# Head norms and first output units moved into the last attention head; convolution taps partly on TensorE, their norm in channel layout

## The reference

```python
def conv_lru_mixer(...):
    h = x @ w_in + b_in                                   # 4 parts of 512: a_val, a_gate, b_gate, b_rec
    ya = silu(layer_norm(causal_depthwise_conv(a_val * sigmoid(a_gate), conv_w, conv_b), cnorm_g, cnorm_b))   # 31 taps
    yb = rg_lru(causal_depthwise_conv(b_rec, lru_conv_w, lru_conv_b), ...) * gelu(b_gate)                   # 4 taps
    return concatenate([ya, yb], axis=-1) @ w_out

def diff_attention_mixer(...):                            # 8 heads, value width 128
    ...                                                   # scores, masked softmax of two maps, p0 - lam * p1, times v
    o = rms_norm(o, subln_g) * (1.0 - lambda_init)        # over the 128 of each head
    return o @ w_out
```

## Time and profile before

| what | value |
|---|---|
| median of 3 runs | 3826.24 us (3825.8 to 3828.29) |
| the profiled execution's own time | 3837.27 us |
| its span | 3835.5 us |
| PE busy | 3571.9 us, 93% |
| DVE, ACT, POOL busy | 48%, 32%, 13% |
| mean granted TensorE clock | 0.95 |

### The profile page before, as it was taken

The page is one execution under the profiler, slowest core; times in us unless marked ns, Lnnn a source line. Parts: engine busy times, 40 slices in busy tenths (PEclk is TensorE's granted clock), DMA queues, the critical chain, the costliest instruction groups (busy, mean ns, idle before and its releaser), DMA issues. The chain is left out here.

```text
span 3835.5 us, 41703 instructions
## 1 busy us (share of the span) xinstructions
PE 3571.9 (93%) x15900; PEld 2867.3 (75%) x15900; DVE 1858.0 (48%) x2465; ACT 1216.6 (32%) x1733; POOL 492.7 (13%) x277
## 2 busy tenths in 40 slices
PE   7847999999998999969999999999988989999998
PEld 5636888888876777638888888888866768888886
DVE  7994623223255666655423233555347865323235
ACT  3225521111133444444411112454422343212123
POOL 0003400000042000006100000442001531000004
PEclk9877999999999999979999999999976989999998
DMA  2101223122122111102222132222221213111113
GB/s 93 38 16 66 88 66 110 52 71 90 48 73 77 45 55 38 38 11 90 91 71 88 49 109 91 96 89 95 72 72 39 82 61 96 58 49 44 49 55 99
DMA packets 75997, 261.14 MB, mean 68 GB/s; under 512 B 10224, under 2 KB 10608, under 8 KB 75888
## 3 DMA queue, kind: packets, MB, share of 16 engines
q1 hardware_dynamic: 75888, 259.69, 21.1%
HBM read 246.54 MB, written 4.72 MB: 66 GB/s over the span
## 5 line engine op out<-in xcount | busy, mean ns | idle before, releaser
L197 PE MATMUL ps<-xh,whi 128*128 128x512 f32 x2880 | 1012.5, 396 | 109.2 <-DVE wlo L628 47.4
L197 PE MATMUL ps<-xl,whi 128*128 128x512 f32 x2880 | 1003.9, 393 | 0.0
L197 PE MATMUL ps<-xh,wlo 128*128 128x512 f32 x2880 | 1002.8, 392 | 0.0
L180 DVE TENSOR_TENSOR wlo<-stage,whi 128x1024 fp32r<-128x1024 f32 x366 | 525.3, 1435 | 507.0 <-ACT whi L174 505.9
L174 ACT ACTIVATE whi<-stage 128x1024 fp32r<-128x1024 f32 x366 | 386.5, 1056 | 1099.6 <-PE ps L197 1068.2
L197 PEld LDWEIGHTS ps<-xh,whi 128*128 128x128 f32 x2880 | 546.9, 190 | 237.0 <-issue 86.2
L197 PEld LDWEIGHTS ps<-xh,wlo 128*128 128x128 f32 x2880 | 546.8, 190 | 115.5
L197 PEld LDWEIGHTS ps<-xl,whi 128*128 128x128 f32 x2880 | 548.2, 190 | 112.7
L197 PE MATMUL ps<-hh,whi 128*128 128x512 f32 x1216 | 422.5, 396 | 5.9 <-ACT lam_t L1477 3.9
L197 PE MATMUL ps<-hl,whi 128*128 128x512 f32 x1216 | 421.2, 395 | 0.0
L197 PE MATMUL ps<-hh,wlo 128*128 128x512 f32 x1216 | 421.2, 395 | 0.0
(11 more groups left out here) (324 smaller groups left out, 3622.9 us busy)
## 6 DMA issues: line engine op xcount, KB each, us to landing
stage<-in_w_ff SPq DMA_DIRECT2D x88, 512.0 KB, 3.5
stage<-in_w_gate SPq DMA_DIRECT2D x59, 512.0 KB, 3.2
stage<-in_w_up SPq DMA_DIRECT2D x59, 512.0 KB, 3.3
stage<-in_w_in SPq DMA_DIRECT2D x50, 512.0 KB, 3.2
ada<-in_w_ada SPq DMA_DIRECT2D x48, 512.0 KB, 3.4
stage<-in_w_qkv SPq DMA_DIRECT2D x43, 512.0 KB, 3.3
stage<-in_w_down SPq DMA_DIRECT2D x48, 448.0 KB, 3.3
stage<-in_w_out SPq DMA_DIRECT2D x32, 512.0 KB, 3.3
```

The source lines that it names most:

```text
L180: dve.tensor_tensor(wlo[slot][:], stage[slot][:], whi[slot][:].bitcast(F32), ALU.subtract).then_inc(w_split, 1)
L197: done = pe.matmul(acc[:, h * HALF:(h + 1) * HALF], wt[slot][:, w], xt[:, b, h * HALF:(h + 1) * HALF], start=b == 0 and wt is whi and xt i ...
```

## The change

In the convolution stage the last 6 taps of each block (in the last block 8 more) become fp32 matmuls with diagonal matrices, which ACT makes from `ident` and the weight columns; the other taps run over all 1024 tokens at a time in two alternating accumulators, and the part from PSUM and the two accumulators are added. The taps are ordered anew, the split of the next block's third unit moves ahead of the scan, and the last block stands outside the loop. `channel_norm` is removed. `ChannelNorm` does the norm for two halves of 512 tokens in channel layout: total, spread_out, deviation, invert and broadcast as in `Norm`, its first half ahead of `out0`, its second half between the first units of `out0` (its totals, its broadcast, and `normalise`, `silu` and `low` on DVE, ACT and POOL). In attention, the block of the head norms is gone. `pe_last`, `act_last` and `dve_last` do the last head, with the norms of heads 0 to 6 and of the first half of head 7, and the first two units of `out1`'s first half between its steps; the low parts go to POOL (`sub_low`). The rest of head 7's norm stands between the units that follow. The three blocks of the program become one.

```diff
-    def channel_norm(name, src, nblk, gain, bias, dst, other):
...
-    TAPS_BEFORE_REC, TAPS_BEFORE_LRU, TAPS_BEFORE_SCAN = 7, 20, 24
+    conv_o = sb("conv_o", [P, S], at=lru_scope)
+    PE_TAPS, LATE_TAPS = 6, 8
+    diag = sb("diag", [P, PE_TAPS, P], at=lru_scope)
+    diag_late = w_gates[:].rearrange("p a k n -> p (a k) n")[:, 0:LATE_TAPS, :]
...
+            def taps_of(i, lo, n, w, to):
+                for t in range(n):
+                    for h in range(2):
+                        at = h * HALF + lo + t
+                        done = pe.matmul(to[:, h * HALF:(h + 1) * HALF], w[:, t, :], a_pad[:, at:at + HALF], start=t == 0, stop=t == n - 1)
+                done.then_inc(tap_mm, 1)
...
-                pe.wait_ge(lru_taps, 2 * LRU_TAPS * i + 2 * LRU_TAPS)
+                pe.wait_ge(diag_ready, i + 1)
+                pe.wait_ge(acc_free, u + 4)
+                taps_of(i, CONV_TAPS - PE_TAPS, PE_TAPS, diag, ps[2])
+                mm_unit(pe, gin0, 2 * i + 1, 1, DB, xh, xl, ready)
+                pe.wait_ge(taps, STEPS * i + WITH_PART + 1)
+                pe.wait_ge(lru_taps, LRU_TAPS * i + LRU_TAPS)
...
+                if last_block(i):
+                    pe.wait_ge(diag_ready, AB + 1)
+                    pe.wait_ge(acc_free, u + 5)
+                    taps_of(i, CONV_TAPS - PE_TAPS - LATE_TAPS, LATE_TAPS, diag_late, ps[0])
...
+            def diagonals(i, lo, n, w):
+                for t in range(n):
+                    done = act.activation(w[:, t, :], ident[:], ACT.Copy, scale=col("conv_w", CONV_TAPS * i + lo + t))
+                done.then_inc(diag_ready, 1)
+            diagonals(0, CONV_TAPS - PE_TAPS, PE_TAPS, diag)
...
+                if last_block(i):
+                    act.wait_ge(gate_w, AB)
+                    diagonals(i, CONV_TAPS - PE_TAPS - LATE_TAPS, LATE_TAPS, diag_late)
+                else:
+                    act.wait_ge(tap_mm, i + 1)
+                    diagonals(i + 1, CONV_TAPS - PE_TAPS, PE_TAPS, diag)
...
+                def conv_steps(n):
+                    for _ in range(n):
+                        k = step[0]
+                        t = k if k < WITH_PART else k - 1
+                        dst = conv_o[:] if k % 2 else out
...
+                        if k == 0:
+                            op = dve.tensor_scalar(dst, a_pad[:, 0:S], col("conv_w", CONV_TAPS * i), col("conv_b", i), ALU.mult, ALU.add)
+                        elif k == 1:
+                            op = dve.tensor_scalar(dst, a_pad[:, 1:1 + S], col("conv_w", CONV_TAPS * i + 1), None, ALU.mult)
+                        elif k == WITH_PART:
+                            dve.wait_ge(tap_mm, i + 1)
+                            op = dve.tensor_tensor(dst, ps[2][:], dst, ALU.add)
+                        else:
+                            op = dve.scalar_tensor_tensor(dst, a_pad[:, t:t + S], col("conv_w", CONV_TAPS * i + t), dst, ALU.mult, ALU.add)
+                        op.then_inc(taps, 1)
+                        step[0] += 1
...
+                conv_steps(6)
...
+                    lru_tap(t)
+                    conv_steps(1)
+                conv_steps(min(SPLIT_AT, n_taps + 1) - step[0])
                 split_lo4(dve, i, 5)
...
+                conv_steps(n_taps + 1 - step[0])
+                done = STEPS * i + n_taps + 1
+                if last_block(i):
+                    dve.wait_ge(decays, 2 * i + 2)
...
+                if not last_block(i):
+                    split_lo4(dve, i, 6)
...
+                    dve.wait_ge(tap_mm, AB + 1)
+                    dve.wait_ge(taps, done + 1)
+                    dve.tensor_tensor(out, ps[0][:], out, ALU.add).then_inc(taps, 1)
...
+        def squares(self, act):
+            for b in range(AB):
+                act.activation(c_sq[:, b, self.t], conv[:, b, self.t], ACT.Square).then_inc(cn_sq, 1)
+        def sums(self, dve):
+            h = self.h
+            for b in range(1, AB):
+                for q, src in enumerate((conv, c_sq)):
+                    to = c_sum[:, h, q, :]
...
+                    dve.tensor_tensor(to, src[:, 0, self.t] if b == 1 else to, src[:, b, self.t], ALU.add).then_inc(cn_sum, 1)
...
+            dst = conv[:, 2 * p:2 * p + 2, self.t]
+            dve.tensor_tensor(dst, dst, wide(BANK_MEAN), ALU.subtract).then_inc(cn_y, 1)
+            dve.wait_ge(cn_y, n + 1)
+            dve.tensor_tensor(dst, dst, wide(BANK_RSTD), ALU.mult).then_inc(cn_y, 1)
...
+        def silu(self, act, p):
+            act.wait_ge(cn_y, 4 * self.h + 2 * p + 2)
+            for b in (2 * p, 2 * p + 1):
+                act.activation(conv[:, b, self.t], conv[:, b, self.t], ACT.Silu, bias=col("cnorm_b", b), scale=col("cnorm_g", b)).then_inc(cn_silu, 1)
+            act.wait_ge(cn_silu, SILU + AB * self.h + 2 * p + 2)
+            act.activation(xh[:, AB + 2 * p:AB + 2 * p + 2, self.t], conv[:, 2 * p:2 * p + 2, self.t], ACT.Copy).then_inc(a_hi, 1)
+        def low(self, eng, p):
+            eng.wait_ge(a_hi, 2 * self.h + p + 1)
+            eng.tensor_tensor(xl[:, AB + 2 * p:AB + 2 * p + 2, self.t], conv[:, 2 * p:2 * p + 2, self.t],
+                              xh[:, AB + 2 * p:AB + 2 * p + 2, self.t].bitcast(F32), ALU.subtract).then_inc(a_lo[self.h], 1)
...
-        run(eng, Head(HEADS - 1), Head(HEADS - 2), False)
...
+    def sub_square(dve, h, k=None):
+        if h == 0:
+            dve.wait_ge(mm_done, gq.base + UPH * HEADS + 2)
+        dve.wait_ge(o_out, NT * h + (NT if k is None else 4 * (k + 1)))
+        o = sub_place(o_t, h, k)
+        dve.tensor_tensor(sub_place(sub_sq_at, h, k), o, o, ALU.mult).then_inc(sub_sq, 1)
+    def sums(pe, h, k):
+        n = 2 * h + k
+        pe.wait_ge(sub_sq, sub_n(h, k if h == HEADS - 1 else None))
...
+        pe.matmul(bank, ones, sub_sq_at[:, h, k * HALF:(k + 1) * HALF], start=True, stop=True).then_inc(sub_mm, 1)
+    def sub_log(act, h, k):
+        act.wait_ge(sub_mm, 2 * h + k + 1)
+        bank = half(ps[0], k) if h < HEADS - 1 else half(ps[0], 1) if k == 0 else half(ps[2], 1)
+        act.activation(sub_rs_at[:, h, k * HALF:(k + 1) * HALF], bank, ACT.Ln, bias=eps[:], scale=1.0 / P).then_inc(sub_ln, 1)
+    def sub_scale(act, h, k=None):
+        act.wait_ge(sub_ln, 2 * h + (2 if k is None else k + 1))
+        r = sub_place(sub_rs_at, h, k)
+        act.activation(r, r, ACT.Exp, scale=-0.5).then_inc(sub_rs, 1)
+    def sub_gain(dve, h, k=None):
+        dve.wait_ge(sub_rs, sub_n(h, k))
+        o = sub_place(o_t, h, k)
+        dve.scalar_tensor_tensor(o, o, lam_t[:, 5:6], sub_place(sub_rs_at, h, k), ALU.mult, ALU.mult).then_inc(sub_o, 1)
+    def sub_high(act, h, k=None):
+        act.wait_ge(sub_o, sub_n(h, k))
+        act.activation(sub_place(xh, h, k), sub_place(o_t, h, k), ACT.Copy).then_inc(sub_hi, 1)
+    def sub_low(eng, h, k=None):
+        eng.wait_ge(sub_hi, sub_n(h, k))
+        eng.tensor_tensor(sub_place(xl, h, k), sub_place(o_t, h, k), sub_place(xh, h, k).bitcast(F32), ALU.subtract).then_inc(sub_lo, 1)
+    def out1_part(pe, u, lo, hi):
+        slot, n = (o1a.base + u) % 2, o1a.base + u
+        if lo == 0:
+            pe.wait_ge(w_split, n + 3)
+            pe.wait_ge(acc_free, n + 1)
+            pe.wait_ge(sub_ln, 2 * (HEADS - 1) + u % 2)
+        for b in range(lo, hi):
+            if u == 0:
+                pe.wait_ge(sub_lo, b + 1)
+            for wt, xt in ((whi, xh), (whi, xl), (wlo, xh)):
+                done = pe.matmul(half(ps[0], u % 2), wt[slot][:, b * P:(b + 1) * P], xt[:, b, 0:HALF],
+                                 start=b == 0 and wt is whi and xt is xh, stop=b == DB - 1 and wt is wlo)
+        if hi == DB:
+            done.then_inc(mm_done, 1)
...
+    def pe_last(pe):
+        def beside(qt, k):
+            if qt in (5, 6):
+                out1_part(pe, qt - 5, 2 * k, 2 * k + 2)
+            if qt == 5 and k == 1:
+                sums(pe, HEADS - 1, 0)
+            if qt == 7 and k < 2:
+                out1_part(pe, k, EARLY_BLOCKS, DB)
+        for qt in range(NT):
+            who, tile = (sixth, NT - 1) if qt == 0 else (last, qt - 1)
+            scores(pe, last, qt)
+            if qt == 1:
+                values_t(pe, last, 1)
+            beside(qt, 0)
+            weights_t(pe, who, tile, 0)
+            beside(qt, 1)
+            weighted(pe, who, tile, 0)
+            if tile >= BATCH:
+                weights_t(pe, who, tile, 1)
+            beside(qt, 2)
+            if tile >= BATCH:
+                weighted(pe, who, tile, 1)
+            if qt == 0:
+                values_t(pe, last, 0)
+            if qt == 1:
+                for h in range(HEADS - 1):
+                    for k in range(2):
+                        sums(pe, h, k)
+        for b in range(2):
+            weights_t(pe, last, NT - 1, b)
+            weighted(pe, last, NT - 1, b)
...
+    def act_last(act):
...
+            if qt == 0:
+                act_values(act, last, 0)
+                split_hi(act, o1a, 0, 1)
+            if qt == 1:
```

(84 more changed lines are left out.)

617 lines of the change are left out of this document (358 added, 259 removed).

## The result

The changed kernel takes **3772.4 us** (median of 4 runs, 3770.9 to 3774.8) against 3826.0 (4 runs, 3825.4 to 3828.3) of the kernel before: ratio 0.9859, 95% interval 0.9842 to 0.9876, 54 us less. The forecast was 3764 in a range of 3745 to 3790, faster with a chance of 0.95. The profiled execution took 3770.9 us, its span is 3769.1. Against the profiled execution of before that is 66 us less, 12 more than the medians say. 11 of them are the excess of that execution of before over its own median, which the forecast took off. It can be placed: past the output product the kernels are the same, and one stretch of 250 us ran at a lower granted clock in the profile of before.

What follows compares the result with a forecast made beforehand. TensorE, busy 93% of the span, was taken as the bound, with gains only where it idles. Gains of 28+17+17 = 62 us from the profiled 3837.3 gave 3775, less 11 for the median of the runs 3764 us; range 3745 to 3790.

Steps and rivals of the forecast that it cites:

- part 3: Last head: head norms and first two output units go between its steps; 54 us removed, 33 added, 4 for GpSimd: gain 17.
- Part 1: Convolution taps: six per block move to TensorE, VectorE does the others at 1024 elements; blocks of 57.2 us, gain 28 us.
- Part 2: Convolution's norm: 44 us removed, 24.5 until the first eviction and 2.9 between units added; gain 17 us, 10 to 20.
- Sums on DVE beside them: Convolution's norm: VectorE's sums lie beside ScalarE's squares and copies, which were counted at 9.6 us with a table.
- the 24.5 of the count: Convolution's norm: forecast time from the stage's end to the first eviction of the output product, 24.5 us.
- The insertions of the second half: Convolution's norm: the second half's sums and broadcast stand between units on TensorE, 1.8+1.1 us.
- the 0.8 us for a meeting of VectorE and GpSimd: Last head: a VectorE split of 1.22 us takes 2.01 beside GpSimd; five such meetings cost 4 us.
- the head eats its gain: Last head: GpSimd's seven subtractions hold up VectorE by 7 x 2 = 14 us, leaving a gain of 3; 3778 us, 20%.
- DVE stays the bound: Convolution blocks: VectorE still sets their length, 60 us a block, 8 us less gain; 3772 us, 17%.
- the change doesn't do what it says: Convolution taps: one at 1024 elements costs twice a half, 1.34 us, 12 us less gain in three blocks; 3776 us, 5%.
- TensorE at 1.2 GHz: Convolution stage: low granted clock slows tap and product matmuls, 62 us more at 0.78, 3984 us at 0.5; 3%.

Runs made afterwards that it cites:

- the rerun: The changed kernel run again without an edit, in another group of runs: median 3776.3 us.
- experiment 8: The changed kernel with 5 or 7 taps of each block on TensorE in place of 6: 3769.4 us with 5, 3780.1 us with 7.
- experiment 3: The changed kernel with GpSimd's four subtractions in the convolution's norm moved behind the twelve sums, 3780.9 us, then behind the reciprocal of the deviation, 3772.5 us.
- experiment 7: The changed kernel with the weight splits of the third and fourth unit moved ahead of the last head's end: 3776.9 us.

## Why the forecast was right

The forecast was 8 us below the result. The convolution's norm and the last head gave 7.1 and 3.0 us less than counted, mostly for one cause, and the convolution stage 2.7 more.

By its number alone the result does not choose the forecast: 3772.4, and 3776.3 in the rerun, lie nearer the rivals' 3772, 3776 and 3778 than 3764, and the range took in all of these. What bears the forecast out is that the three parts and their mechanism (TensorE as the new bound of a block, the norm's chain, the head's growth) are seen in the trace. That the sum came out so close is partly luck, as two errors of opposite sign met in part 3.

- **Part 1, 28 us forecast, 30.7 measured.** The tap instructions take 10.47/24 = 0.44 us, as taken from the gates' row, blocks are 57.3 us apart (57.2), and TensorE is the bound, shown by experiment 8. The last block was forecast to end at 262.4 and ended at 260.0: ScalarE's table for the gelu now loads in its wait for TensorE, and the gate value is there at 248.2, not 250.3.
- **Part 2, 17 forecast, 9.9 measured.** "Sums on DVE beside them" was the step that failed. The sums lie beside GpSimd's four subtractions and cost 8.6 us more. With these moved, 25.6 us lie between the stage's end and the first eviction, against the 24.5 of the count. The insertions of the second half cost 2.7 (2.9). In the rerun's profile, with the granted clock at 0.50 until 299 us, they cost 5.8 and the whole part gives 5.6.
- **Part 3, 17 forecast, 14.0 measured.** By the starts of the maxima, tile 0 grew by 9.8 us (10 forecast) and tile 1 by 13.3 (14). Tiles 2 to 4 grew by 17.3 (6 and most of the 4 for GpSimd); without the 10.5 of hold-ups that is 6.8. Tiles 5 to 7 shrank by 1.5 (3 longer forecast), as the final products took 2.07 us at the lower clock before and 1.16 now. So the step that failed was the 0.8 us for a meeting of VectorE and GpSimd: 4 us were counted and 10.5 measured. The 4.5 us by which tiles 5 to 7 beat their forecast hid most of it, for a reason that was not counted; the head grew by 38.8 us against 37 (33 and 4). The other 1.3 us lie behind the head: the third unit took 8.3 us and not 5.4, as its first half ran at a granted clock of 0.55.
- **The error behind both** was a reading of one row: a split that took 2.01 in place of 1.22 was taken as the price of a meeting. It is the price of what was left of a short instruction of GpSimd. That stood in the trace of before: GpSimd's instruction of 1.31 us started at 340.93, the split at 341.31, so it had 0.9 us to go, and the split took 0.8 longer. Beside a longer one, in the changed kernel, 1.9 us are to go and the split takes 1.7 longer:

```profile
340.93 1.31 POOL L459 TENSOR_TENSOR sum_a<-x 128x512 f32<-128x512 f32 x1 [39.31 <-DVE x L586]
```

```profile
317.06 2.96 DVE L180 TENSOR_TENSOR wlo<-stage,whi 128x1024 fp32r<-128x1024 f32 x1 [0.47 <-ACT whi L174]
316.54 2.39 POOL L869 TENSOR_TENSOR xl<-conv,xh 128x1024 fp32r<-128x1024 f32 x1
```

  The rule of the Trainium skill ("SBUF — State Buffer", SBUF: two separate sides), a shared port locked for a whole instruction with the loser blocked, gave the right size for a hold-up: 2.1 to 2.2 us. As a forecast for the head it overshoots (17 us for seven subtractions), since only five VectorE operations (four gains, one half square) were held up in the head; the rival "the head eats its gain" (3778) had this mechanism, but its price of 14 stood for 10.5, and the 3 us that it left this part stood for 14.0. In part 2 neither the forecast nor a rival had it.
- **DVE stays the bound**, **the change doesn't do what it says** (taps of 1024 at 1.34) and **TensorE at 1.2 GHz** are ruled out by the blocks: 57.3 us at a granted clock of 1.00, so that 3772 and 3776, the numbers of the first two, are met by coincidence. The higher price of a table change that the Trainium skill ("ScalarE: Activation LUTs", What ACT_TABLE_LOAD costs) gives did not show: the load ahead of the 14 logarithms starts at 1598.43, takes 1.28 us, and the first logarithm starts at 1599.72.

## What to carry to other kernels

Before work is put beside GpSimd, list every VectorE operation there that reads nothing from PSUM, tiny ones included, and count each at what is left of GpSimd's instruction, up to the whole of it; put GpSimd where VectorE reads PSUM or waits. When an engine's queue gets work of another stage, put what is ready ahead of what waits for a third engine (6.2 us for a swap of two lines). When work is moved between two engines that are nearly balanced, try one unit fewer and one more: one tap was worth 1.7 us a block.

## What the runs showed of the hardware that was not expected

- The hold-up doesn't scale with the held-up operation: 128x4 took 2.2 us in place of 0.16, 128x512 2.8 in place of 0.69. It also hit an operation with a single tensor operand in SBUF (the third long row of experiment 3). GpSimd pays too, less: 12.19/4 = 3.0 and 2.64 us a subtraction in contention, 9.33/4 = 2.3 beside VectorE operations that read PSUM.
- The clock comes back at different moments in executions of the same code. Behind the norm, in which TensorE is busy for 8.8 of 22 us (262 to 284) at a granted clock of 0.53, the second unit of the output product takes 7.2 us in the changed kernel's first profile and 10.3 in its second. Busy time by stretch, first and second:

```profile
291.00:299.00 8.00, 8.00 (x47) 6.95 (x46) 2.98 (x8) 3.41 (x5) 0.00 (x0) 1.00 0.20 68
```

```profile
293.00:299.00 6.00, 6.00 (x24) 5.42 (x23) 2.75 (x7) 3.16 (x4) 0.00 (x0) 0.50 0.25 87
```

  A wait of 2.8 us ahead of a unit cost 5.5 for the same reason (experiment 7).
